# Gate slots of six output tiles: one 512-column matmul for the high weights times [high | low] operand

## The chip, the cores and the metric

The kernel runs on one core of a Trainium2 chip. The metric is device time in microseconds (us) of one execution, median over runs; lower is better. Engines are called by the profile's short names: PE (TensorE, the matmuls), PEld (its weight loads), DVE (VectorE), ACT (ScalarE), POOL (GpSimd) and SP (SyncE, which issues the weight DMAs here). They run side by side and meet at semaphores. TensorE reads SBUF and writes PSUM; DVE and ACT read and write both; POOL works in SBUF.

## The reference, cut to what matters

Two small transformer blocks on 256 tokens of width 1024. The part that the change touches closes the first block's state-space mixer:

```python
    g = jax.nn.gelu(y).astype(h.dtype)
    val, gate = jnp.split(g @ w_glu, 2, axis=-1)
    return val * jax.nn.sigmoid(gate)
...
            x = x + s5_mixer(h, ssm_w_in[i], ...)
        h = rms_norm(x, ffn_norm[i])
        x = x + conv_ffn(h, ffn_w_up[i], ffn_conv_w[i], ffn_conv_b[i], ffn_w_down[i])
```

All of it is fp32. `w_glu` is 1024 x 2048.

## The kernel before

Activations lie transposed: 128 features on the partitions, 256 tokens along the row, eight such tiles (`m` or `k` from 0 to 7) for the 1024 features. All weights come as one stream of 197 slots of 128 x 2048 floats, through a ring of six buffers that SP fills well ahead. A slot holds 16 blocks of 128 x 128 (8 `k` times 2 output halves).

A product in full precision is made of three products of reduced precision (fp32r). ACT rounds the slot into `w_hi` (`high_part`, line 503, one 128x2048 Copy). POOL subtracts that from the slot to get `w_lo` (`low_part`, line 413, four pieces of 128x512), and then tells `w_ready`. The operand is split in the same way into `hi` and `lo`. For each block PE runs `three` (lines 1568 to 1570): `w_hi`*hi, `w_lo`*hi and `w_hi`*lo, 256 columns each, all added into one PSUM bank; that is 48 matmuls a slot. `w_hi` and `w_lo` have three buffers each (`SPLIT`).

The gate stage has slots 4 to 11, one for each output tile: slot 4+m holds the value columns of tile m as half 0 and its gate columns as half 1. Slot 4 is handled whole, slots 5 to 11 with `three`. Slot 5's low part is made by DVE; POOL's first one is slot 6. Slot 12 is the first of the feed-forward stage (ffn0). The order on each engine is written out by hand. In the gate loop, for tile m:

- ACT runs the Copy for `w_hi` of slot 4+m+2 (`high_parts_to(s + 2)`), waits until PE is done with slot 4+m, takes the sigmoid of the gate half (line 650), and waits for `x_ready`. Then `operand_tile` makes the next stage's `hi` tile (line 641) and the square (line 642), and the loop goes on to the next tile's Copy.
- DVE waits for `gated`, multiplies value by sigmoid (line 1158: one input in PSUM, one in SBUF), adds the product to `x` (line 1160: both inputs in SBUF, tells `x_ready`), and makes the `lo` tile (line 972, all in SBUF).
- POOL makes the low part of a slot when ACT's Copy of it has ended; PE starts a slot when its low part is done (`w_ready`) and the slot before it has ended.

In tile 1, ACT also issues a small DMA (`bias_oh`) ahead of the sigmoid; behind slot 8, PE has a small product for the bias table. In tile 7, ACT loads another function table and makes `w_hi` of slot 14 between the sigmoid and the operand tile. Behind the loop it issues the load of `p0` and splits it (`pe_operand`) before it comes to ffn0's norm.

Of the kernel before, what the change touches and what calls it, by code (L numbers as in the profile page):

```python
# [9 lines left out]
P = 128  # L10
D = 1024
T = 256
KT = D // P
# [24 lines left out]
for _name, _n in STAGES:  # L38
# [8 lines left out]
SET = dict(s5=1, ffn0=0, ple0=0, q=1, kv=0, diff=1, ffn1=0, ple1=0, even=1, mixed=1,  # L47
           ffn2=0, odd=0, stick=1, ffn3=0)
# [31 lines left out]
def stick_pair(t):  # L80

    return STICK_AT.index(t) if t in STICK_AT else None
# [97 lines left out]
def program(nc, a, out):  # L180
    f32, f32r = mybir.dt.float32, mybir.dt.float32r
    ALU, ACT, AX = mybir.AluOpType, mybir.ActivationFunctionType, mybir.AxisListType
    ctx = ExitStack()
    with ctx:
        def sb(name, shape, dt=f32):
            return ctx.enter_context(nc.sbuf_tensor(name, shape, dt))
# [16 lines left out]

        with nc.sbuf_tensor("s5_cm", [P, 2, 2, PAIRS, 32], f32) as s5_cm:
            pass
        opnd = [sb("opnd0", [P, 2, KT, T], f32r)]
        opnd.append(sb("opnd1", [P, 2, KT, T], f32r))
        acc = ctx.enter_context(nc.psum_tensor("acc", [P, 4, 512], f32))
        up = [ctx.enter_context(nc.psum_tensor(f"up{i}", [P, 2, T], f32)) for i in range(2)]
        side = ctx.enter_context(nc.psum_tensor("side", [P, 2, 512], f32))  # L210
# [15 lines left out]
        def sem(name):  # L226
            if name not in sems:
                sems[name] = ctx.enter_context(nc.semaphore(name))
            return sems[name]
# [89 lines left out]
        def weights_hi(s):  # L319

            return last_hi[s] if s in last_hi else w_hi[:, s % SPLIT]

        def weights_lo(s):

            return last_lo[s] if s in last_lo else w_lo[:, s % SPLIT]
# [18 lines left out]
        def hi(name):  # L344
            return opnd[SET[name]][:, 0]

        def lo(name):
            return opnd[SET[name]][:, 1]

        block = ctx.enter_context(nc.Block())  # L350

# [125 lines left out]
        def _(act):  # L477
            c = Counts(act, sem)
            A = nc.scalar.activation
# [25 lines left out]
            def high_parts_to(s):  # L505
                while ahead[0] <= min(s, N_SLOTS - 1):
                    high_part(ahead[0])
                    ahead[0] += 1
# [8 lines left out]
            def root_tables():  # L517

                nc.scalar.preload_act_table_set("natural_log_exp_and_others")
# [18 lines left out]
            w = s_small  # L538
# [100 lines left out]
            def operand_tile(name, m):  # L639
                c.wait("x_ready")  # L640
                c.up(A(hi(name)[:, m], x[:, m], ACT.Copy, scale=gain(name, m)), "hi_ready")  # L641
                c.up(A(sq[:, m], x[:, m], ACT.Square), "sq_ready")

            for m in range(KT):
                s = START["glu"] + m
                high_parts_to(s + 2)
                act.wait_ge(sem("mm_done"), s + 1)
                if m == 1:
                    act.dma_start(d_oh, a["bias_oh"]).then_inc(dma["bias_oh"], 16)
                c.up(A(f_gg[:, 0], up[m % 2][:, 1], ACT.Sigmoid), "gated")  # L650
                if m == KT - 1:
                    root_tables()
                    high_parts_to(s + 3)
                operand_tile("ffn0", m)
# [89 lines left out]
            S = START["kvq"]  # L744
# [69 lines left out]
            S = START["evin"]  # L814
# [61 lines left out]
            for n in range(EVEN_STEPS):  # L876
# [16 lines left out]
                if n >= 5 and n % 2:  # L893
                    h = (n - 5) // 2
# [11 lines left out]
            S = START["qkv"]  # L906
# [5 lines left out]
            for t in range(STICK_HALVES):  # L912
# [16 lines left out]
                p = stick_pair(t - 1)  # L929
# [7 lines left out]
                p = stick_pair(t - 3)  # L937
# [5 lines left out]
                p = stick_pair(t - 1)  # L943
# [7 lines left out]
                p = stick_pair(t - 4)  # L951
# [10 lines left out]
        def _(dve):  # L962
            c = Counts(dve, sem)
            V = nc.vector

            def step(ins):
                c.up_and_wait(ins, "dve_step")

            def low_tile(name, m):

                c.wait("hi_ready")
                c.up(V.scalar_tensor_tensor(lo(name)[:, m], x[:, m], gain(name, m), hi(name)[:, m].bitcast(f32),  # L972
                                            ALU.mult, ALU.subtract), "lo_ready")
# [9 lines left out]
            w = s_small  # L983
# [170 lines left out]


            for m in range(KT):
                c.wait("gated")
                step(V.tensor_tensor(f_h[:, 0], up[m % 2][:, 0], f_gg[:, 0], ALU.mult))
                c.tell("up_free")
                c.up_and_wait(V.tensor_tensor(x[:, m], x[:, m], f_h[:, 0], ALU.add), "x_ready")  # L1160
                low_tile("ffn0", m)
                if m == 5:
                    c.wait("bias_ps")
                    c.up_and_wait(V.tensor_copy(d_row, aux[0][0:HEADS, 0:384]), "bias_sb")
# [132 lines left out]
            S, u0 = START["kvq"], BANK["kvq"]  # L1297
# [81 lines left out]
            S, u0 = START["evin"], BANK["evin"]  # L1379
# [88 lines left out]
            for n in range(EVEN_STEPS):  # L1468
# [12 lines left out]
                if n >= 6 and n % 2 == 0:  # L1481
                    h = (n - 6) // 2
# [9 lines left out]
            S, u0 = START["qkv"], BANK["qkv"]  # L1492
# [19 lines left out]
            for t in range(STICK_HALVES):  # L1512
# [4 lines left out]
                p = stick_pair(t - 1)  # L1517
# [6 lines left out]
                p = stick_pair(t - 3)  # L1524
# [7 lines left out]
                p = stick_pair(t - 2)  # L1532
# [7 lines left out]
                p = stick_pair(t - 4)  # L1540
# [9 lines left out]
        def _(pe):  # L1550
            c = Counts(pe, sem)
            MM = nc.tensor.matmul
            used = [0]

            def slot_ready(s, i=None):
                pe.wait_ge(sem("w_ready"), s + 1 if i is None else i * 6 + (s + 1))

            def bank(i=None, loop_uses=0):

                u = used[0]  # L1560
                used[0] += 1
                if u >= 2:
                    pe.wait_ge(sem("up_free"), u - 1 if i is None else i * 4 + (u - 1))
                return up[u % 2]

            def three(o, l_hi, l_lo, r_hi, r_lo, start, stop):

                MM(o, l_hi, r_hi, start=start, stop=False, skip_group_check=True)  # L1568
                MM(o, l_lo, r_hi, start=False, stop=False, skip_group_check=True)  # L1569
                return MM(o, l_hi, r_lo, start=False, stop=stop, skip_group_check=True)  # L1570

            def square_sums(h):

                c.wait("sq_ready", KT // 2)
                for q in range(4):
                    ins = MM(aux[1][QUAD * q:QUAD * q + QUAD, 0:T], ones[:, 0:QUAD], sq[:, 4 * h + q],  # L1576
                             start=(h == 0), stop=(h == 1), tile_position=(0, QUAD * q), skip_group_check=True)
                if h:
                    c.up(ins, "ssq")
# [21 lines left out]
            def up_slot(name, s, i=None, fresh=False, sums=False, fold=False, tokens=0, order=range(KT)):  # L1601

                slot_ready(s, i)
                o = bank(i)
                w_h, w_l = weights_hi(s), weights_lo(s)
                for j, k in enumerate(order):
                    if fresh:
                        c.wait("hi_ready")
                        c.wait("lo_ready")
                    for m in range(2):  # L1610
                        w = slice((2 * k + m) * P, (2 * k + m + 1) * P)
                        ins = three(o[:, m], w_h[:, w], w_l[:, w], hi(name)[:, k], lo(name)[:, k],
                                    k == order[0] and m == 0, k == order[-1])
                    if sums and j == KT // 2 - 1:
                        square_sums(0)
                    between(k, fold, tokens)
                c.up(ins, "mm_done")
                if sums:
                    square_sums(1)

            def begin_slot(s):
                slot_ready(s)
                return bank()
# [71 lines left out]
            S = START["w_in"]  # L1695
# [30 lines left out]
            o = whole_bank(S)  # L1726
# [4 lines left out]
            for m in range(KT):  # L1731
                c.wait("sq_ready")
                ins = MM(aux[1][:, 0:T], ones, sq[:, m], start=(m == 0), stop=(m == KT - 1), skip_group_check=True)
# [65 lines left out]
            o = whole_bank(S + 1)  # L1799
# [6 lines left out]
            o = whole_bank(S + 2)  # L1806
# [9 lines left out]
            o = whole_bank(S + 3)  # L1816
# [10 lines left out]
            S = START["glu"]  # L1827
# [11 lines left out]
            o = whole_bank(S)  # L1839
# [1 line left out]
            s5_out(7)  # L1841
            gelu_part(o, range(4, KT))
            for m in range(1, KT):
                up_slot("s5", S + m, fresh=(m == 1))
                if m == 4:
                    pe.wait_ge(dma["bias_oh"], 16)
                    c.up(MM(aux[0][0:HEADS, 0:384], d_oh[:, 384:384 + HEADS], d_oh[:, 0:384], start=True, stop=True),
                         "bias_ps")
# [50 lines left out]
            S = START["kvq"]  # L1899
# [86 lines left out]
            for t in range(DIFF_HALVES):  # L1986
                i, half = t // 2, t % 2
                if i < 12:
                    if half == 0:
                        o = begin_slot(S + i)  # L1990
# [20 lines left out]
            S = START["evin"]  # L2011
# [125 lines left out]
            S = START["qkv"]  # L2137
# [83 lines left out]
            for t in range(STICK_HALVES):  # L2221
                i, half = t // 2, t % 2
                if i < 12:
                    if half == 0:
                        o = begin_slot(S + i)
# [9 lines left out]
                p = stick_pair(t - 3)  # L2235
                if p is not None:
                    stick_values(p)
                p = stick_pair(t)
# [153 lines left out]
```

## Time and profile before

| | |
|---|---|
| median of 3 runs | 1327.33 us (1327.25 to 1328.0) |
| profiled execution, first to last instruction | 1324.4 us |
| instructions | 27666 |
| PE busy | 1296.3 us, 98% of the span |
| POOL busy | 1006.1 us, 76% |
| ACT busy | 682.9 us, 52% |
| DVE busy | 637.0 us, 48% |
| mean granted TensorE clock | 0.999 of full speed |

The profiled execution is one of its own: its span is 2.9 us shorter than the median run, since a run's time also holds what lies around the instructions. Busy shares are means over stages with different limits. A row of the timeline gives start and length in us from the span's start; a matmul's length is its own latency, and matmuls overlap, so what one costs is read from the distance of starts.

### The profile page before, as it was taken

Reading aid. Unit: us, or ns where it says so; the run is one execution under the profiler, and the core shown is the slowest. Engines: PE = TensorE matmul, PEld = TensorE weight load, DVE = VectorE, ACT = ScalarE, POOL = GpSimd, SP = SyncE. Lnnn points to the kernel's source line nnn. Section 1 sums busy time; section 2 is a strip of 40 time slices with the busy share of each in tenths; the row PEclk is TensorE's granted clock in tenths of the full one; section 3 lists DMA queues with packets and bytes.
Section 4 is the critical chain, followed back from the end, with each engine's and each line's share of the span. In section 5 each row is a group of like instructions: output and inputs, shape, how many; then the busy total and the mean of one; then the engine's idle time right before and its main releaser. Section 6 shows DMA issues by size and latency. Waiting matters only on the chain.

```text
span 1324.4 us, 27666 instructions
## 1 busy us (share of the span) xinstructions
PE 1296.3 (98%) x10976; PEld 1247.4 (94%) x10976; DVE 637.0 (48%) x1163; ACT 682.9 (52%) x944; POOL 1006.1 (76%) x793
## 2 busy tenths in 40 slices
PE   6999999999999999999999999999999999999999
PEld 6889999999988889999999978999999999999998
DVE  8994465555555748455565574211113455311112
ACT  7725643444666756443457565434446566543342
POOL 1327888888777659888887794988887766988885
PEclk9999999999999999999999999999999999999999
DMA  6305675545535235555454532555554433555530
GB/s 269 129 33 181 169 250 191 185 172 181 191 134 185 101 126 183 178 188 188 172 178 160 193 128 96 192 192 179 174 185 167 160 126 120 187 178 187 190 127 32
DMA packets 33879, 217.07 MB, mean 164 GB/s; under 512 B 3683, under 2 KB 7428, under 8 KB 8196
## 3 DMA queue, kind: packets, MB, share of 16 engines
q1 hardware_dynamic: 30096, 211.14, 45.1%
q10 hardware_dynamic: 3700, 4.75, 1.4%
q8 instruction: 60, 0.98, 0.3%
q14 instruction: 23, 0.19, 0.0%
HBM read 213.26 MB, written 2.62 MB: 163 GB/s over the span
## 4 chain that ended last, share of the span: by engine, by line
PE 85%; DVE 6%; ACT 6%; issue 2%; POOL 1%; DMA 0%; DVEq 0%; SPq 0%; ACTq 0%; POOLq 0%
PE up L1568 19%; PE up L1569 18%; PE up L1570 18%; PE acc L1568 7%; PE acc L1570 6%; PE acc L1569 6%; DVE opnd L972 2%; PE side L1795 2%; PE up L1703 1%; PE acc L1761 1%; ACT w_hi L503 1%; ACT opnd L641 1%; PE side L1576 1%; PE up L1834 1%; PE acc L1933 0%
## 5 line engine op out<-in xcount | busy, mean ns | idle before, releaser
L413 POOL TENSOR_TENSOR w_lo<-ring,w_hi 128x512 fp32r<-128x512 f32 x748 | 955.4, 1311 | 235.7 <-ACT w_hi L503 231.8
L1568 PE MATMUL up<-opnd,w_hi 128*128 128x256 f32 x2064 | 592.3, 287 | 3.7 <-DVE opnd L972 1.5
L1569 PE MATMUL up<-opnd,w_lo 128*128 128x256 f32 x2064 | 583.9, 283 | 0.0
L1570 PE MATMUL up<-opnd,w_hi 128*128 128x256 f32 x2064 | 583.8, 283 | 0.0
L503 ACT ACTIVATE w_hi<-ring 128x2048 fp32r<-128x2048 f32 x188 | 358.9, 1910 | 264.4 <-PE up L1570 202.7
L1568 PEld LDWEIGHTS up<-opnd,w_hi 128*128 128x128 f32 x2064 | 395.6, 192 | 16.1 <-issue 13.1
L1569 PEld LDWEIGHTS up<-opnd,w_lo 128*128 128x128 f32 x2064 | 395.8, 192 | 1.3 <-issue 1.0
L1570 PEld LDWEIGHTS up<-opnd,w_hi 128*128 128x128 f32 x2064 | 395.7, 192 | 0.0
L1568 PE MATMUL acc<-opnd,w_hi 128*128 128x256 f32 x784 | 223.0, 284 | 1.2 <-DVE x L1218 1.2
L1569 PE MATMUL acc<-opnd,w_lo 128*128 128x256 f32 x784 | 221.8, 283 | 0.0
L1570 PE MATMUL acc<-opnd,w_hi 128*128 128x256 f32 x784 | 221.8, 283 | 0.0
L1568 PEld LDWEIGHTS acc<-opnd,w_hi 128*128 128x128 f32 x784 | 150.4, 192 | 2.8 <-DVE x L1218 2.1
L1569 PEld LDWEIGHTS acc<-opnd,w_lo 128*128 128x128 f32 x784 | 150.4, 192 | 0.0
L1570 PEld LDWEIGHTS acc<-opnd,w_hi 128*128 128x128 f32 x784 | 150.4, 192 | 0.0
L977 DVE TENSOR_TENSOR side<-up,rstd 128x512 f32<-128x512 f32 x44 | 30.8, 699 | 198.9 <-PE up L1570 189.9
L977 DVE TENSOR_TENSOR mix<-up,rstd 128x512 f32<-128x512 f32 x72 | 49.7, 691 | 144.3 <-PE up L1570 116.0
L664 ACT ACTIVATE opnd<-side 128x256 fp32r<-128x256 f32 x88 | 33.8, 384 | 110.6 <-DVE side L1198 110.6
L972 DVE SCALAR_TENSOR_TENSOR opnd<-x,par,opnd 128x256 fp32r<-128x256 f32 x80 | 66.9, 855 | 24.3 <-ACT opnd L641 19.5
L1198 DVE TENSOR_TENSOR side<-mix,side 128x256 f32<-128x256 f32 x88 | 37.7, 429 | 71.3 <-ACT mix L662 67.0
L1201 DVE TENSOR_TENSOR opnd<-side,opnd 128x256 fp32r<-128x256 f32 x88 | 37.4, 425 | 46.0 <-ACT opnd L664 46.0
L662 ACT ACTIVATE mix<-side 128x256 f32<-128x256 f32 x88 | 33.0, 375 | 51.2 <-DVE side L1189 47.7
L427 POOL TENSOR_TENSOR s_work<-s_work 128x512 f32<-128x512 f32 x7 | 8.9, 1277 | 66.0 <-DVE s_work L1119 35.4
(296 smaller groups left out, 1421.3 us busy)
## 6 DMA issues: line engine op xcount, KB each, us to landing
ring<-in_stream SPq DMA_DIRECT2D x197, 1024.0 KB, 4.9
bias_rows<-mix ACTq DMA_DIRECT2D x1, 1536.0 KB
mix<-in_s_b SPq DMA_DIRECT2D x1, 1024.0 KB, 5.6
x<-in_x SPq DMA_DIRECT2D x1, 1024.0 KB, 7.7
mix<-in_s_c SPq DMA_DIRECT2D x1, 1024.0 KB, 11.7
mix<-bias_rows ACTq DMA_DIRECT2D x1, 1024.0 KB, 5.4
out_x<-x SPq DMA_DIRECT2D x8, 128.0 KB, 1.7
mix<-in_p ACTq DMA_DIRECT2D x2, 256.0 KB, 3.4
```

Source lines behind the costliest of these rows:

```text
L413: ins = nc.gpsimd.tensor_tensor(w_l[:, cols], ring[:, r, cols], w_h[:, cols].bitcast(f32), ALU.subtract)
L503: c.up(A(weights_hi(s), ring[:, s % RING], ACT.Copy), "w_hi_ready")
L662: c.up(A(f_gg[:, 0], gate_ps, ACT.Gelu_apprx_tanh if l < 2 else ACT.Silu), "gated")
L664: c.up(A(opnd[1][:, 0, 2 * parity + part], h_ps, ACT.Copy), "h_hi")
L972: c.up(V.scalar_tensor_tensor(lo(name)[:, m], x[:, m], gain(name, m), hi(name)[:, m].bitcast(f32), ALU.mult, ALU.subtract), "lo_ready")
L977: c.up_and_wait(V.tensor_tensor(dst, up[u][:], rstd[:].unsqueeze(1).broadcast_to([P, 2, T]), ALU.mult), "up_free")
L1198: c.up_and_wait(V.tensor_tensor(h_ps, f_gg[:, 0], val_ps, ALU.mult), "h_raw")
L1201: c.up_and_wait(V.tensor_tensor(hl, h_ps, hh.bitcast(f32), ALU.subtract), "h_ready")
L1568: MM(o, l_hi, r_hi, start=start, stop=False, skip_group_check=True)
L1569: MM(o, l_lo, r_hi, start=False, stop=False, skip_group_check=True)
L1570: return MM(o, l_hi, r_lo, start=False, stop=stop, skip_group_check=True)
L1795: ins = MM(o, s5_cm[:, r, 1 - odd, pair], rhs, start=False, stop=(k == 3), tile_position=(0, 32 * q), skip_group_check=True)
```

## The change

For tiles 1 to 6 (slots 5 to 10), the two products with `w_hi` become one: hi and lo of an operand tile now lie side by side (`both`, 512 columns), and one matmul multiplies `w_hi` with the pair. Its left 256 columns hold `w_hi`*hi, to which `w_lo`*hi is added as before; the right 256 columns hold `w_hi`*lo by itself. So each half of a slot takes a whole PSUM bank (of `acc`, in place of a half of `up`), and the two halves of a result still have to be added. ACT copies the right halves of both banks to SBUF (128x512, `f_c[:, 0:2]`), DVE adds the left halves to them (128x512, to `f_c[:, 2:4]`), and ACT's sigmoid and DVE's multiply then read that sum. Tiles 0 and 7 stay as they were.

```diff
-        opnd = [sb("opnd0", [P, 2, KT, T], f32r)]
-        opnd.append(sb("opnd1", [P, 2, KT, T], f32r))
+        both = [sb("opnd0", [P, KT, 2, T], f32r)]
+        both.append(sb("opnd1", [P, KT, 2, T], f32r))
+        opnd = [v.rearrange("p k h t -> p h k t") for v in both]
...
+        def hi_lo(name):
+            return both[SET[name]]
+
+        def glu_banks(m):
+
+            return acc[:, 2 * (m % 2):2 * (m % 2) + 2]
...
-                c.up(A(f_gg[:, 0], up[m % 2][:, 1], ACT.Sigmoid), "gated")
+                if 0 < m < KT - 1:
+                    c.up(A(f_c[:, 0:2], glu_banks(m)[:, :, T:2 * T], ACT.Copy), "cross_sb")
+                    c.wait("glu_sum")
+                    c.up(A(f_gg[:, 0], f_c[:, 3], ACT.Sigmoid), "gated")
+                else:
+                    c.up(A(f_gg[:, 0], up[m % 2][:, 1], ACT.Sigmoid), "gated")
...
-                c.wait("gated")
-                step(V.tensor_tensor(f_h[:, 0], up[m % 2][:, 0], f_gg[:, 0], ALU.mult))
-                c.tell("up_free")
+                if 0 < m < KT - 1:
+                    c.wait("cross_sb")
+                    c.up_and_wait(V.tensor_tensor(f_c[:, 2:4], glu_banks(m)[:, :, 0:T], f_c[:, 0:2], ALU.add), "glu_sum")
+                    c.tell("up_free")
+                    c.wait("gated")
+                    step(V.tensor_tensor(f_h[:, 0], f_c[:, 2], f_gg[:, 0], ALU.mult))
+                else:
+                    c.wait("gated")
+                    step(V.tensor_tensor(f_h[:, 0], up[m % 2][:, 0], f_gg[:, 0], ALU.mult))
+                    c.tell("up_free")
...
+            def wide_slot(s, o, fresh=False):
+
+                slot_ready(s)
+                bank()
+                w_h, w_l = weights_hi(s), weights_lo(s)
+                for k in range(KT):
+                    if fresh:
+                        c.wait("hi_ready")
+                        c.wait("lo_ready")
+                    for m in range(2):
+                        w = slice((2 * k + m) * P, (2 * k + m + 1) * P)
+                        MM(o[:, m, 0:T], w_l[:, w], hi("s5")[:, k], start=(k == 0), stop=False, skip_group_check=True)
+                        ins = MM(o[:, m], w_h[:, w], hi_lo("s5")[:, k], start=False, stop=(k == KT - 1),
+                                 skip_group_check=True)
+                c.up(ins, "mm_done")
...
-                up_slot("s5", S + m, fresh=(m == 1))
+                if m < KT - 1:
+                    wide_slot(S + m, glu_banks(m), fresh=(m == 1))
+                else:
+                    up_slot("s5", S + m)
```

On ACT, one turn of the gate loop was, from the Copy of a slot's weights to the next one (slots 8 and 9; `mix` is the memory in which `f_gg` and `f_c` lie):

```order
79 L503 ACTIVATE w_hi<-ring 128x2048
80 L650 ACTIVATE mix<-up 128x256
81 L641 ACTIVATE opnd<-x,par 128x256
82 L642 ACTIVATE sq<-x 128x256
83 L503 ACTIVATE w_hi<-ring 128x2048
```

and is now this (line numbers of the changed kernel are 8 to 20 higher on ACT and DVE):

```order
85 L511 ACTIVATE w_hi<-ring 128x2048 [waits mm_done,ring_full2]
86 L659 ACTIVATE mix<-acc 128x512 [waits mm_done]
87 L661 ACTIVATE mix<-mix 128x256 [waits glu_sum]
88 L649 ACTIVATE opnd<-x,par 128x256 [waits x_ready]
89 L650 ACTIVATE sq<-x 128x256
90 L511 ACTIVATE w_hi<-ring 128x2048 [waits mm_done,ring_full3]
```

One instruction of 512 columns and a wait for DVE (`glu_sum`) have come in ahead of the sigmoid; the next slot's Copy (line 511, before 503) still stands behind all of it.

On DVE a tile was:

```order
135 L1158 TENSOR_TENSOR mix<-up,mix 128x256 [waits gated]
136 L1160 TENSOR_TENSOR x<-x,mix 128x256 [waits dve_step]
137 L972 SCALAR_TENSOR_TENSOR opnd<-x,par,opnd 128x256 [waits hi_ready,x_ready]
```

and is now:

```order
135 L1172 TENSOR_TENSOR mix<-acc,mix 128x512 [waits cross_sb]
136 L1175 TENSOR_TENSOR mix<-mix 128x256 [waits glu_sum,gated]
137 L1180 TENSOR_TENSOR x<-x,mix 128x256 [waits dve_step]
138 L985 SCALAR_TENSOR_TENSOR opnd<-x,par,opnd 128x256 [waits hi_ready,x_ready]
```

There is an addition more, and the multiply (line 1175) now reads only `mix`, which is SBUF, where it read `up`, which is PSUM.

## Rows read from the trace of the kernel before

**Rows 1.** Page, the chain that ended last: shares of the span by engine

```profile
PE 85%; DVE 6%; ACT 6%; issue 2%; POOL 1%; DMA 0%; DVEq 0%; SPq 0%; ACTq 0%; POOLq 0%
```

**Rows 2.** Busy time in a stretch: length, then PE, PEld, DVE, ACT, POOL, clock, DMA

```profile
106.00:130.00 24.00, 24.00 (x197) 23.77 (x196) 8.93 (x12) 14.18 (x18) 22.41 (x17) 1.00 0.61 222
```

**Rows 3.** Timeline of PE, starts of gate slots: start, length, line, operation

```profile
107.03 0.28 PE L1569 MATMUL up<-opnd,w_lo 128*128 128x256 f32 x1
107.15 0.28 PE L1570 MATMUL up<-opnd,w_hi 128*128 128x256 f32 x1
...
124.18 0.28 PE L1568 MATMUL up<-opnd,w_hi 128*128 128x256 f32 x1
...
148.15 0.28 PE L1568 MATMUL up<-opnd,w_hi 128*128 128x256 f32 x1
```

**Rows 4.** Timeline of ACT in the gate stage; in brackets the idle time before

```profile
110.62 1.90 ACT L503 ACTIVATE w_hi<-ring 128x2048 fp32r<-128x2048 f32 x1
...
113.47 0.38 ACT L650 ACTIVATE mix<-up 128x256 f32<-128x256 f32 x1 [0.95 <-PE up L1570]
115.46 0.51 ACT L641 ACTIVATE opnd<-x,par 128x256 fp32r<-128x256 f32 x1 [1.60 <-DVE x L1160]
...
116.18 1.90 ACT L503 ACTIVATE w_hi<-ring 128x2048 fp32r<-128x2048 f32 x1
118.62 0.38 ACT L650 ACTIVATE mix<-up 128x256 f32<-128x256 f32 x1 [0.54 <-PE up L1570]
```

**Rows 5.** Timeline of DVE in the gate stage

```profile
113.89 0.42 DVE L1158 TENSOR_TENSOR mix<-up,mix 128x256 f32<-128x256 f32 x1 [2.59 <-ACT mix L650]
114.47 0.95 DVE L1160 TENSOR_TENSOR x<-x,mix 128x256 f32<-128x256 f32 x1 [0.15 <-DVE mix L1158]
...
119.62 1.38 DVE L1160 TENSOR_TENSOR x<-x,mix 128x256 f32<-128x256 f32 x1 [0.15 <-DVE mix L1158]
```

**Rows 6.** Timeline of POOL, single pieces of the low parts

```profile
112.60 1.29 POOL L413 TENSOR_TENSOR w_lo<-ring,w_hi 128x512 fp32r<-128x512 f32 x1
113.84 1.30 POOL L413 TENSOR_TENSOR w_lo<-ring,w_hi 128x512 fp32r<-128x512 f32 x1
115.09 1.48 POOL L413 TENSOR_TENSOR w_lo<-ring,w_hi 128x512 fp32r<-128x512 f32 x1
...
120.67 1.48 POOL L413 TENSOR_TENSOR w_lo<-ring,w_hi 128x512 fp32r<-128x512 f32 x1
```

**Rows 7.** Timeline of PE, two fp32r matmuls of 512 columns and what follows

```profile
1066.56 0.63 PE L2187 MATMUL acc<-mix_r 128*128 128x512 f32 x2
1067.03 0.39 PE L2189 MATMUL acc<-mix_r 128*128 128x256 f32 x2
```

**Rows 8.** Groups by line and shape, DVE: count, busy us, mean ns, idle before

```profile
L1160 DVE TENSOR_TENSOR x<-x,mix 128x256 f32<-128x256 f32 x8 | 7.6, 947 | 1.2 <-DVE mix L1158 1.2
...
L1530 DVE TENSOR_TENSOR mix<-mix,acc 128x512 f32<-128x512 f32 x8 | 5.5, 688 | 4.7 <-PE acc L2191 4.7
...
L1346 DVE SCALAR_TENSOR_TENSOR mix<-mix 128x256 f32<-128x256 f32 x8 | 3.9, 484 | 0.3
...
L1158 DVE TENSOR_TENSOR mix<-up,mix 128x256 f32<-128x256 f32 x8 | 3.4, 424 | 21.5 <-ACT mix L650 21.5
```

**Rows 9.** Groups by line and shape, ACT: a 512-column Copy out of PSUM

```profile
L575 ACT ACTIVATE s_work<-acc 64x512 f32<-64x512 f32 x4 | 2.4, 592 | 3.5 <-PE acc L1719 3.4
```

**Rows 10.** Timeline of ACT at the end of the gate stage

```profile
148.35 0.38 ACT L650 ACTIVATE mix<-up 128x256 f32<-128x256 f32 x1 [1.25 <-PE up L1570]
...
150.04 0.36 ACTq L734 DMA_DIRECT2D mix<-in_p  x1
150.04 1.91 ACT L503 ACTIVATE w_hi<-ring 128x2048 fp32r<-128x2048 f32 x1
...
151.86 0.49 ACT L641 ACTIVATE opnd<-x,par 128x256 fp32r<-128x256 f32 x1
...
154.26 0.72 ACT L698 ACTIVATE opnd<-mix 128x256 fp32r<-128x256 f32 x2 [1.60 <-DMA mix<-in_p]
```

## The prediction

> **What bounds the kernel now.** I read the chain that ended last first: 85% of the span is PE [rows 1], so the kernel ends when PE's matmuls do. The stretch of the gate slots comes next, because a mean says nothing of a stage: from 106 to 130 us PE is busy all the time at the full clock, but POOL is busy 22.41 us of 24.00 too [rows 2]. PE is ahead of the others by a little only, and the question is by how much.
>
> PE's pace: matmuls of 256 columns start 0.12 us apart (107.03, 107.15), so a slot of 48 lasts 5.76 us. Slot 8 starts at 124.18 and slot 12 at 148.15 [rows 3], and nothing but a small product for the bias table stands between.
>
> How weights come to PE: ACT's Copy of slot 7 ends at 110.62 + 1.90 = 112.52 [rows 4], POOL's first piece of it starts at 112.60 [rows 6], 0.08 us later. So POOL waits for ACT, slot by slot. ACT's Copy of slot 8 ends at 116.18 + 1.90 = 118.08 [rows 4]; four pieces, two at 1.25 us from start to start (112.60 to 113.84) and two at 1.44, make 5.4, so slot 8's low part is ready near 123.55, only 0.6 us before PE starts on it at 124.18. I call T(s) the end of ACT's Copy of slot s; w_ready(s) is T(s) + 5.5. That 0.6 us is all that the gate loop of ACT can lose before PE waits.
>
> What ACT's loop consists of: for tile 1, sigmoid at 113.47, operand tile at 115.46, Copy of slot 8 at 116.18 [rows 4]. In the 1.6 us between the first two it waits for DVE: multiply 0.42 (113.89), 0.15 for its own semaphore, addition to `x` 0.95 (114.47) [rows 5].
>
> Why that addition takes 0.95 or 1.38 us: POOL's pieces. It ends at 115.42, which is 0.33 behind the start of a POOL piece at 115.09; the one that starts at 119.62 ends at 121.00, again 0.33 behind a piece, at 120.67 [rows 5, 6]. And these pieces take 1.48 us, not 1.29. So a DVE instruction with both inputs in SBUF waits for the end of the POOL piece that runs, goes between two pieces, and lengthens the next by 0.19. The groups say the same: mean 947 ns for the addition (line 1160), 424 for the multiply that has one input in PSUM (line 1158), 484 for a two-SBUF-input instruction in a stage where POOL rests (line 1346) [rows 8]. The Trainium skill, "SBUF — State Buffer", section "SBUF: two separate sides", has this rule: GpSimd and a VectorE instruction with two SBUF inputs take one port pair as an exclusive lock for a whole instruction. By that rule, the trace agrees.
>
> **The change, part by part.** *PE.* Two matmuls of 256 columns go, one of 512 comes. Two fp32r matmuls of 512 columns occupy 1066.56 to 1067.03, 0.235 us each [rows 7], against 2 x 0.12 = 0.24 [rows 3]. A slot of 16 blocks falls from 5.76 to 16 x (0.12 + 0.235) = 5.68 us, at most 0.5 us over six slots. PE pays by column, so one weight load fewer is worth almost nothing.
>
> *ACT and DVE, per tile of 1 to 6.* New, ahead of the sigmoid: a Copy of 512 columns out of PSUM, 0.59 us (line 575, half the partitions [rows 9]; not under the 0.38 that 256 columns take [rows 4]), and DVE's addition of 512 columns with one input in PSUM, 0.69 (line 1530 [rows 8]), with about 0.04 us at each hand-over (sigmoid's end 113.85 to multiply at 113.89 [rows 4, 5]). That is 1.36 us on the chain. The multiply stays 256 wide, but now reads `f_c` and `f_gg`, both in SBUF, so it falls under the wait for POOL's piece, as line 1160 does. Then the addition to `x` comes 0.15 us after it, inside the next piece, and waits for that one's end as well.
>
> *One turn of ACT's loop, from T on.* An ACT instruction behind another starts 0.09 before that one's listed end (151.86 against 150.04 + 1.91 [rows 10]). Copy -0.09 to 0.50; addition 0.54 to 1.23; sigmoid 1.27 to 1.67 (0.38 from PSUM; I take 0.40 from SBUF); multiply ready at 1.71. POOL's pieces start at 0.08, 1.33 and 2.58, so the multiply waits until 2.58 and ends 2.90. Addition to `x` ready at 3.05; the third piece, lengthened, ends the wait at 4.02, and it is done at 4.34. Operand tile 4.38; the next Copy starts 0.72 later (115.46 to 116.18 [rows 4]), at 5.10, and ends at 7.00. **The loop takes 7.0 us a tile, and PE needs 5.68.** ACT, not PE, sets the pace, and POOL follows it (5.5 of 7.0). What is queued behind the wait on ACT is the Copy of the next slot's weights, and POOL and then PE wait for that.
>
> *Tile 1.* T(7) = 112.52 stays. Copy at 113.47 to 114.06, addition to 114.79, sigmoid to 115.23, multiply ready at 115.27: just behind the piece that starts at 115.09 [rows 6], so it waits for 116.34 and ends 116.66. Addition to `x` from 116.81: that piece ends 117.78, done 118.10; operand tile 118.14, Copy 118.86, T(8) = 120.76 instead of 118.08. PE's slot 6 is done by then (sigmoid at 118.62 before [rows 4]), so ACT goes on without a pause: T(9) = 127.76, T(10) = 134.76, T(11) = 141.76, T(12) = 148.76, T(13) = 155.76.
>
> *PE.* Slot 8 starts at T(8) + 5.6 = 126.4 (was 124.18), slot 12 at 154.4 (was 148.15): **6.2 us late**. In between PE idles 1.3 us a slot, and the shorter slots only lengthen that; the 0.5 us buys nothing. Slot 5's own start, and ACT's, are as before.
>
> *Behind it.* Tile 7's sigmoid comes at 155.7 instead of 148.35, 7.3 late, so the DMA of `p0`, issued 1.7 us behind it, lands, and its split (154.26 [rows 10]) runs, 7.3 late where PE is 6.2 late. ACT's norm stands behind that split, so between 0 and 1.1 us come on top; I take 0.4, because before the change the norm could wait some tenths without PE noticing. From there PE bounds as before (98% busy over the span), and nothing gives time back.
>
> *Sum.* 6.2 + 0.4 = 6.6 us. The profiled span would go from 1324.4 to 1331.0; the median of runs is 2.9 above the span, so 1327.3 + 6.6 = **1333.9 us**.
>
> *Bounds.* The Copy may cost 0.38 to 0.68; in the steady turn the multiply is then ready between 1.50 and 1.80, still between the pieces at 1.33 and 2.58, so the period doesn't move: waits come in steps of a piece. In tile 1 it decides: 0.18 us quicker and the multiply catches 115.09, T(8) is 1.25 earlier, and the sum 5.0 to 5.4. Above: with the whole 1.1 from `p0`, 7.3. Case by case 1332.3 to 1334.6.
>
> **The rivals.** *A: the multiply isn't held by POOL* (its place is line 1175 of the changed kernel, its price 0.42). Then the addition to `x` is ready at 2.28 and catches 2.58; the period is 5.56, under PE's 5.68. In tile 1, T(8) is 119.3, slot 8's low part is ready at 124.85, 0.7 late; later slots don't wait, and six shorter slots take back up to 0.4: +0.3 to +0.5, **1327.7**, no slowdown that shows. It decides at the second piece that is waited for. Against it: line 1160 at 947 ns against 424 with PSUM. For it: its two inputs and its output lie close together in one tile, which I have no row for. 10%.
>
> *B: in part.* The multiply finds POOL idle or catches the first piece in some of the tiles, as hand-overs are shorter than 0.04 us or pieces lie otherwise: some tiles at 5.75, others at 7.0; three of six gives about +3, **1330.3**. 9%.
>
> *C: faster.* The 512-column matmul costs no more than one of 256 and the new steps are hidden. Then a slot takes 16 x 0.24 = 3.84 us, but PE can't have slot 11 ahead of its low part, which before came 2.1 us ahead of PE: **1325.2**. That is hardly 0.2% and needs rival A too. The Trainium skill, "TensorE: Matmul & The Clock Gate", section "Back-to-back issue gap", speaks for such a price, with about 131 ns for 512 columns in a stream against 81 for 128. The fp32r matmuls here take 235 [rows 7], and the measurement decides. 2%.
>
> *D: more.* One more piece waited for in each turn, or a slow clock in PE's new pauses: 6 x 1.25 = 7.5 on top, **1341**. 4%.
>
> **How the numbers follow.** The forecast, ACT's loop as the bound in all six tiles, has 75%. The range 1330.0 to 1336.5 holds it, most of B, and up to 2.6 us of further pauses above; it leaves out A, C, D and a little of B, some 18%. About 0.2% (2.65 us) is what a measurement of this kernel can tell from no change. Faster by more than that: 1%. Within: A, nearly all of C, a third of B, 14%. Slower: the rest, 85%.
>
> **What would show it.** In the profile after: the wide matmul and the next start 0.235 us apart; PE's idle time in the gate stage is ended by POOL's low part, about 1.3 us a slot from slot 8 on; ACT's Copies of slots 8 to 13 end 7.0 us apart; line 1175 takes 0.9 to 1.2 us and ends 0.33 behind the start of a POOL piece, and so does line 1180; slot 12 starts 6.2 us later. I am wrong if line 1175 takes 0.42, or if ACT's Copies follow PE's pace, or if the time lost at slot 12 comes back in ffn0.

## The result and the profile after

| | median | runs |
|---|---|---|
| before, same chip | 1327.29 us | 4 (1326.36 to 1328.0) |
| changed kernel | 1333.31 us | 4 (1332.82 to 1334.16) |

The ratio is 1.0047 (95% interval 1.0033 to 1.0061): the change costs 6.0 us. The forecast was 1333.9. The profiled execution has a span of 1332.4 us and is the longest of the four (1334.16 us); 8.0 us lie between the two spans, 6.0 between the medians. A run's time is 1.8 us above its own span here, so of the 2.9 us between span and median before the change only 1.8 lies around the instructions: the execution profiled before was a short one, and it stands against a long one.

The page first. The chain of work that ended last, and the group of POOL's low parts (count, busy us, mean ns; then the idle time before them and what ended it):

```profile
PE 83%; DVE 8%; ACT 6%; issue 2%; POOL 1%; DMA 0%; DVEq 0%; ACTq 0%; SPq 0%; POOLq 0%
...
L421 POOL TENSOR_TENSOR w_lo<-ring,w_hi 128x512 fp32r<-128x512 f32 x748 | 954.9, 1310 | 243.8 <-ACT w_hi L511 240.8
```

PE gives two hundredths of the chain to DVE [rows 1]. POOL's idle time ahead of the low parts is 243.8 us where it was 235.7, and what ACT's Copy ended of it 240.8 where it was 231.8. Over the whole kernel PE is busy about as long as before (1298.9 us against 1296.3), so shares can't say where 6 us went. The waits of PE from 107 to 165 us can (total, times, longest):

```profile
PE acc L1652 <- POOL w_lo L421: 2.2, 1, 2.2
PE up L1588 <- POOL w_lo L421: 2.0, 2, 1.1
PE up L1588 <- DVE opnd L985: 1.1, 1, 1.1
```

In the kernel before this list is empty for the stage. Three of the four waits are for a slot's low part, which is what the prediction said; the fourth, for tile 7's operand, it did not see. The places in the timeline of PE (start, length of one):

```profile
124.20 0.40 PE L1653 MATMUL acc<-opnd,w_hi 128*128 128x512 f32 x1
126.76 0.52 PE L1652 MATMUL acc<-opnd,w_lo 128*128 128x256 f32 x1 [2.16 <-POOL w_lo L421]
...
147.72 0.39 PE L1588 MATMUL up<-opnd,w_hi 128*128 128x256 f32 x1 [1.05 <-POOL w_lo L421]
...
154.71 0.39 PE L1588 MATMUL up<-opnd,w_hi 128*128 128x256 f32 x1 [0.98 <-POOL w_lo L421]
...
160.48 0.28 PE L1590 MATMUL up<-opnd,w_hi 128*128 128x256 f32 x1
161.88 0.36 PE L1588 MATMUL up<-opnd,w_hi 128*128 128x256 f32 x1 [1.12 <-DVE opnd L985]
```

Slot 8 starts at 126.76, slot 11 at 147.72, slot 12 at 154.71, where the kernel before had 124.18 and 148.15 for slots 8 and 12 [rows 3]. Gate slot 5 began at 106.72 before and at 107.21 here (0.49 later, ahead of all that the change touches), so slot 12 is (154.71 - 107.21) - (148.15 - 106.72) = 6.07 us late. Behind it one pause more: 161.88 - 160.48 = 1.40 us between two starts that otherwise lie 0.12 apart, 1.28 lost. 0.49 + 6.07 + 1.28 = 7.84 of the 8.0 us between the spans.

Why the low parts are late is one turn of ACT's loop. The chain of work in order of time, from 119 to 128 us (start, us on the chain):

```profile
119.05 0.40 ACT sq L650
119.45 1.81 ACT w_hi L511
121.26 0.48 ACT mix L659
121.75 0.02 issue
121.77 0.70 DVE mix L1172
122.47 0.02 issue
122.50 0.43 ACT mix L661
122.92 0.02 issue
122.95 1.23 DVE mix L1175
124.18 0.02 issue
124.20 1.39 DVE x L1180
125.59 0.02 issue
125.61 0.03 ACT opnd L649
125.64 0.39 issue
126.03 0.40 ACT sq L650
126.43 1.80 ACT w_hi L511
```

No PE and no POOL stand in it: weights for slot 8 (L511), the new Copy (L659), the new addition (L1172), sigmoid, multiply (L1175), addition to `x` (L1180), squares of the operand tile, and then L511 again at 126.43, 6.98 us after the last. The chain of this stretch used to be PE matmul behind PE matmul. Now look at POOL in the same stretch, single pieces:

```profile
122.59 1.29 POOL L421 TENSOR_TENSOR w_lo<-ring,w_hi 128x512 fp32r<-128x512 f32 x1
123.84 1.46 POOL L421 TENSOR_TENSOR w_lo<-ring,w_hi 128x512 fp32r<-128x512 f32 x1
```

The multiply could begin at 122.95 and ends at 122.95 + 1.22 = 124.17, 0.33 behind the start of the piece at 123.84; that piece is long (1.46) as the lengthened ones of before were [rows 6]. Before, the multiply had one input in PSUM and took 0.42 [rows 5].

### The profile page after: what moved, and what is told of

Read it like the earlier page. It is cut to its first block, busy times and chain, and to the rows that moved or that the text cites. A ratio compares the mean times of both kernels' runs of the same rounds, so it can differ in the third digit from the quotient of the medians.

```text
span 1332.4 us, 27486 instructions
## 1 busy us (share of the span) xinstructions
PE 1298.9 (97%) x10880; PEld 1244.0 (93%) x10880; DVE 647.8 (49%) x1169; ACT 685.9 (51%) x950; POOL 1005.7 (75%) x793
## 4 chain that ended last, share of the span: by engine, by line
PE 83%; DVE 8%; ACT 6%; issue 2%; POOL 1%; DMA 0%; DVEq 0%; ACTq 0%; SPq 0%; POOLq 0%
PE up L1588 18%; PE up L1589 17%; PE up L1590 17%; PE acc L1588 7%; PE acc L1590 6%; PE acc L1589 6%; PE up L1739 2%; DVE opnd L985 2%; ACT w_hi L511 2%; PE side L1831 2%; PE acc L1797 1%; ACT opnd L649 1%; PE side L1596 1%; PE up L1870 1%; PE acc L1972 0%
## 5 line engine op out<-in xcount | busy, mean ns | idle before, releaser
L421 POOL TENSOR_TENSOR w_lo<-ring,w_hi 128x512 fp32r<-128x512 f32 x748 | 954.9, 1310 | 243.8 <-ACT w_hi L511 240.8
L1588 PE MATMUL up<-opnd,w_hi 128*128 128x256 f32 x1968 | 565.1, 287 | 6.8 <-DVE opnd L985 2.6
L1589 PE MATMUL up<-opnd,w_lo 128*128 128x256 f32 x1968 | 556.7, 283 | 0.0
L1590 PE MATMUL up<-opnd,w_hi 128*128 128x256 f32 x1968 | 556.6, 283 | 0.0
L511 ACT ACTIVATE w_hi<-ring 128x2048 fp32r<-128x2048 f32 x188 | 358.9, 1910 | 264.5 <-PE up L1590 202.9
L1588 PEld LDWEIGHTS up<-opnd,w_hi 128*128 128x128 f32 x1968 | 377.2, 192 | 19.3 <-issue 13.7
L1589 PEld LDWEIGHTS up<-opnd,w_lo 128*128 128x128 f32 x1968 | 377.4, 192 | 1.2 <-issue 1.0
L1590 PEld LDWEIGHTS up<-opnd,w_hi 128*128 128x128 f32 x1968 | 377.3, 192 | 0.0
L985 DVE SCALAR_TENSOR_TENSOR opnd<-x,par,opnd 128x256 fp32r<-128x256 f32 x80 | 67.3, 860 | 24.5 <-ACT opnd L649 19.4
```

The costliest lines, as they stand in the source:

```text
L421: ins = nc.gpsimd.tensor_tensor(w_l[:, cols], ring[:, r, cols], w_h[:, cols].bitcast(f32), ALU.subtract)
L511: c.up(A(weights_hi(s), ring[:, s % RING], ACT.Copy), "w_hi_ready")
```

## The experiments

Two batches; in the first the kernel before took 1326.66 us (27 runs, 1326.01 to 1327.85), in the second 1326.88 (21 runs, 1326.05 to 1327.62). "Late" below is read at one row that all kernels have, the norm's first sums over `sq` in slot 12, counted from slot 5's start; before, that distance is 151.12 - 106.72 = 44.40 us.

| kernel | median us (runs) | ratio, 95% interval | norm's sums less slot 5 | late |
|---|---|---|---|---|
| new layout alone | 1326.59 (10) | 1.0000 (0.9991 to 1.0009) | 152.16 - 107.78 | 0.0 |
| wide matmul split | 1334.48 (4) | 1.0058 (1.0042 to 1.0073) | 158.70 - 108.14 | 6.2 |
| sum in PSUM | 1328.55 (11) | 1.0013 (1.0004 to 1.0022) | 153.35 - 107.41 | 1.5 |
| sum in PSUM, weights first | 1326.58 (11) | 0.9999 (0.9990 to 1.0008) | 151.50 - 107.89 | -0.8 |
| changed kernel again | 1333.38 (4) | 1.0054 (1.0039 to 1.0070) | 156.30 - 106.86 | 5.0 |
| weights first | 1326.43 (10) | 0.9999 (0.9990 to 1.0008) | 151.63 - 108.03 | -0.8 |
| half pieces | 1330.08 (10) | 1.0025 (1.0015 to 1.0034) | 154.39 - 107.03 | 3.0 |
| tile 7's operand first | 1333.12 (5) | 1.0049 (1.0035 to 1.0062) | 156.35 - 106.86 | 5.1 |

**The new layout alone**, in the kernel before: hi and lo side by side, three matmuls as ever.

```diff
-        opnd = [sb("opnd0", [P, 2, KT, T], f32r)]
-        opnd.append(sb("opnd1", [P, 2, KT, T], f32r))
+        both = [sb("opnd0", [P, KT, 2, T], f32r)]
+        both.append(sb("opnd1", [P, KT, 2, T], f32r))
+        opnd = [v.rearrange("p k h t -> p h k t") for v in both]
```

> The kernel before with the operands' new layout alone (hi and lo of a tile side by side); no instruction more or less. My theory (the changed kernel loses its 6 us because ACT's gate loop takes 7.0 us a tile, as DVE's multiply and addition each wait for a POOL piece) expects no change: 1327.3 us, within 2 us, PE's slots 5.76 us. A rival, that the new layout costs PE or DVE something at every use of the operands, expects a good part of the 6 us here: 1330 us or more.

1326.59 against 1326.66 us: the layout costs nothing.

**The wide matmul split** in the changed kernel: the same sums in the same banks and the same work on ACT and DVE, but two matmuls of 256 columns.

```diff
-                        ins = MM(o[:, m], w_h[:, w], hi_lo("s5")[:, k], start=False, stop=(k == KT - 1),
+                        MM(o[:, m, 0:T], w_h[:, w], hi("s5")[:, k], start=False, stop=(k == KT - 1), skip_group_check=True)
+                        ins = MM(o[:, m, T:2 * T], w_h[:, w], lo("s5")[:, k], start=False, stop=(k == KT - 1),
                                  skip_group_check=True)
```

> The changed kernel with its 512-column matmul split again into two of 256 columns with the same weights; banks, Copy, additions and order stay. My theory says that PE isn't what is waited for in these slots, so the time stays that of the changed kernel, 1333.3 us, within 1.5 us, with ACT's Copies still 7.0 us apart and less idle time on PE. A rival, that the wide matmul is what slows PE (pauses, or a slow clock), expects a return towards 1327; one that it saves PE time that counts expects 1334 or more.

1334.48 us, no faster than the change, and as late in slot 12: ACT's Copies are 6.96 to 7.00 us apart from tile 2 on, and PE waits for low parts at the same three places (1.9 us in one, 1.9 in two, where it was 2.2 and 2.0). So the form of PE's work isn't what makes slot 12 late; what is left for that is on ACT and DVE. By the time alone the rival that put 1334 or more on a saving of PE isn't excluded: the median is 1.1 to 1.2 us above those of the changed kernel, and the intervals overlap. In the profile it isn't seen: the spans lie 0.9 us apart (1333.3 and 1332.4), and slot 5 already starts 0.93 later (108.14 and 107.21), ahead of everything in which the two kernels differ.

**The sum in PSUM**: DVE's addition writes over the left halves of the banks, and sigmoid and multiply read them there. As many instructions of the same sizes, but the multiply has one input in PSUM again.

```diff
-                    c.up(A(f_gg[:, 0], f_c[:, 3], ACT.Sigmoid), "gated")
+                    c.up(A(f_gg[:, 0], glu_banks(m)[:, 1, 0:T], ACT.Sigmoid), "gated")
...
-                    c.up_and_wait(V.tensor_tensor(f_c[:, 2:4], glu_banks(m)[:, :, 0:T], f_c[:, 0:2], ALU.add), "glu_sum")
-                    c.tell("up_free")
+                    sums = glu_banks(m)[:, :, 0:T]
+                    c.up_and_wait(V.tensor_tensor(sums, sums, f_c[:, 0:2], ALU.add), "glu_sum")
                     c.wait("gated")
-                    step(V.tensor_tensor(f_h[:, 0], f_c[:, 2], f_gg[:, 0], ALU.mult))
+                    step(V.tensor_tensor(f_h[:, 0], glu_banks(m)[:, 0, 0:T], f_gg[:, 0], ALU.mult))
+                    c.tell("up_free")
```

> The changed kernel, but DVE's 512-column addition leaves its sum in PSUM, so that the sigmoid and the multiply read PSUM, and the multiply again has one input there; Copy, addition and their hand-overs all stay. My theory: the multiply takes 0.42 us and waits for no piece of POOL; the loop falls from 7.0 to 5.56 us, a little under PE's slot of 5.6; tile 1 still costs some 1 us, and the shorter slots give some tenths back: 1327.3 to 1328.2 us, and a multiply of 0.42 us in the profile. The rival, that the Copy and the addition on the chain (1.4 us a tile) are what costs and not the multiply's wait, expects 1331 to 1333.

1328.55 us, 1.9 above the kernel before: most of the cost is gone, and this is what separates the theory from a cost of the added instructions as such. The timeline of its DVE in the turn of tile 2:

```profile
120.54 0.70 DVE L1173 TENSOR_TENSOR acc<-acc,mix 128x512 f32<-128x512 f32 x1 [1.74 <-ACT mix L659]
121.77 0.42 DVE L1175 TENSOR_TENSOR mix<-acc,mix 128x256 f32<-128x256 f32 x1 [0.52 <-ACT mix L661]
122.35 0.58 DVE L1181 TENSOR_TENSOR x<-x,mix 128x256 f32<-128x256 f32 x1 [0.16 <-DVE mix L1175]
```

The multiply takes 0.42 where the change took 1.22, and the addition to `x` is in time for the end of the piece in which the multiply ran (0.58 where it was 1.38). ACT's Copies of weights start at 111.31, 118.13, 123.69, 129.25, 136.03, 142.84 and 148.41, which is 5.56 apart or 6.8: a turn catches a piece or waits for one more. PE waits twice for low parts, 0.8 us each; I put the 0.35 us above the expected range down to the turns of 6.8, on the profile's word alone.

The Trainium skill, "SBUF — State Buffer", section "SBUF: two separate sides", words it as an exclusive lock on the port pair that GpSimd and a VectorE instruction with two SBUF inputs share, held for a whole instruction. The two kernels bear it out from both sides: 1.22 us with two inputs in SBUF, 0.42 with one in PSUM, same shape, same place.

**The sum in PSUM, weights first**: besides, ACT makes the next slot's weights between its Copy and its wait for DVE's sum.

```diff
                     c.up(A(f_c[:, 0:2], glu_banks(m)[:, :, T:2 * T], ACT.Copy), "cross_sb")
+                    high_parts_to(s + 3)
                     c.wait("glu_sum")
```

> As the kernel that leaves the sum in PSUM, and ACT makes the high part of the next slot between its 512-column Copy and the sigmoid, not behind the operand tile. My theory: the Copy for the next weights no longer waits for DVE, POOL runs ahead of PE, ACT's turn is 4.9 us, and PE's slots of some 5.6 us set the pace: six slots shorter by 0.1 to 0.2 us, 1326.2 to 1327.0 us, and no idle time of PE ended by POOL's low part in slots 7 to 11. A rival, that PE itself is slower in wide slots, expects 1328 or more.

1326.58 us, no difference from before, with all of the new work still there. PE waits nowhere in the stage, and POOL has one row for 32 pieces:

```profile
108.21 43.09 POOL L421 TENSOR_TENSOR w_lo<-ring,w_hi 128x512 fp32r<-128x512 f32 x32 [18.23 <-ACT w_hi L511]
```

Slot 12's row comes 0.8 us earlier than before. Slots 7, 9 and 10 take 5.64 to 5.66 us from one to the next where three matmuls of 256 columns took 5.76, so I read this as PE's own saving; no run takes it apart from the rest. A median with an interval of 0.2% can't show it.

**The changed kernel again**, in the second batch, unedited.

> The changed kernel once more, as the measure for the three beside it. Expected 5.5 to 7.5 us over the kernel before, as measured already (6.0 by the medians).

1333.38 us, the same. Its profile differs in tile 1 from the first one, and this was one of the bounds of the prediction. DVE's multiply and POOL's piece behind it here:

```profile
115.24 0.42 DVE L1175 TENSOR_TENSOR mix<-mix 128x256 f32<-128x256 f32 x1 [0.48 <-ACT mix L661]
```
```profile
115.26 1.56 POOL L421 TENSOR_TENSOR w_lo<-ring,w_hi 128x512 fp32r<-128x512 f32 x1
```

and in the first profile of the same kernel:

```profile
115.59 1.59 DVE L1175 TENSOR_TENSOR mix<-mix 128x256 f32<-128x256 f32 x1 [0.48 <-ACT mix L661]
```
```profile
115.61 1.29 POOL L421 TENSOR_TENSOR w_lo<-ring,w_hi 128x512 fp32r<-128x512 f32 x1
```

In both the multiply came 0.02 us ahead of the piece's listed start; once it went first, once it waited out the piece, at 1.17 us. What decides between the two, the listed times don't show. From there on both run at 7.0 us a turn (ACT's Copies at 117.86, 124.85, 131.86, 138.84, 145.82, 152.81 here), one 1.1 us behind the other at slot 12.

**Weights first**, with the sum in SBUF as in the change.

```diff
                     c.up(A(f_c[:, 0:2], glu_banks(m)[:, :, T:2 * T], ACT.Copy), "cross_sb")
+                    high_parts_to(s + 3)
                     c.wait("glu_sum")
```

> The changed kernel, with ACT's high part of the next slot moved between the 512-column Copy and the sigmoid; the sum stays in SBUF and the multiply still waits for a POOL piece. My theory: that wait then delays x, hi and lo, but not the weights; POOL runs ahead of PE, ACT's turn is about 6.3 us against PE's 5.6, so tile 7's operand comes some 3 us late and PE waits for it once, at the end of ffn0's first slot: 1.2 to 2.5 us over the kernel before. The rival, that the multiply's wait costs PE directly by its length wherever it stands, expects 4 us or more over it.

Missed: 1326.43 us, as before the change, where I expected a cost. I had taken the multiply's wait to stay as it was and to lengthen the turn. The rows of ACT and DVE:

```profile
120.66 1.91 ACT L511 ACTIVATE w_hi<-ring 128x2048 fp32r<-128x2048 f32 x1
...
126.24 1.91 ACT L511 ACTIVATE w_hi<-ring 128x2048 fp32r<-128x2048 f32 x1
```
```profile
122.90 0.67 DVE L1176 TENSOR_TENSOR mix<-mix 128x256 f32<-128x256 f32 x1 [1.42 <-ACT mix L662]
123.61 1.40 DVE L1181 TENSOR_TENSOR x<-x,mix 128x256 f32<-128x256 f32 x1
```
```profile
123.25 1.48 POOL L421 TENSOR_TENSOR w_lo<-ring,w_hi 128x512 fp32r<-128x512 f32 x1
...
124.68 1.48 POOL L421 TENSOR_TENSOR w_lo<-ring,w_hi 128x512 fp32r<-128x512 f32 x1
...
126.12 1.48 POOL L421 TENSOR_TENSOR w_lo<-ring,w_hi 128x512 fp32r<-128x512 f32 x1
```

Both DVE instructions are still held: they end at 123.57 and 125.01, 0.32 and 0.33 behind the pieces at 123.25 and 124.68. But no weights stand behind them, POOL never pauses (one row of 32 pieces, 44.19 us), and a turn is 5.58 us, which is four pieces of POOL, three of them lengthened (1.25 from start to start, and 1.43 or 1.44 three times: the operand tile's low part is held too). Two later turns take 6.1 and 6.3 us, and PE still waits nowhere. Since POOL no longer starts afresh at T(s), the multiply doesn't meet its pieces where it did; here it falls near the end of one. So a held DVE instruction costs here only what is queued behind it.

**Half pieces**: POOL makes the low parts of slots 6 to 13 in eight pieces of 256 columns, nothing else in the change is touched. If the wait is for a piece, it must shrink with the piece.

```diff
-                for q in range(QUARTERS):
-                    cols = slice(q * 2048 // QUARTERS, (q + 1) * 2048 // QUARTERS)
+                n = 2 * QUARTERS if START["glu"] <= s < START["ffn0"] + 2 else QUARTERS
+                for q in range(n):
+                    cols = slice(q * 2048 // n, (q + 1) * 2048 // n)
```

> The changed kernel, with POOL's low parts of slots 6 to 13 in eight pieces of 256 columns, not four of 512. My theory: each of DVE's two waits ends at the next piece, so they shrink by about 0.6 us each at most; ACT's Copies come about 5.9 us apart, not 7.0, if POOL's pieces take about 0.7 us: 1 to 3 us over the kernel before. If a piece of 256 columns takes 0.75 us or more, POOL itself needs 6 us a slot and it is 3 us or more. The rival, that DVE's multiply and addition are slow for another reason than the piece that runs (two SBUF inputs as such), expects no gain: 5.5 us or more over it, and line 1175 as long as before.

1330.08 us, 3.2 over the kernel before: half of the cost. In the turn of tile 2 the multiply takes 0.80 where it took 1.22, and still ends 0.33 behind the start of a piece (121.63 + 0.80 = 122.43 against 122.10):

```profile
121.63 0.80 DVE L1176 TENSOR_TENSOR mix<-mix 128x256 f32<-128x256 f32 x1 [0.48 <-ACT mix L662]
122.46 0.85 DVE L1181 TENSOR_TENSOR x<-x,mix 128x256 f32<-128x256 f32 x1
```
```profile
121.41 0.74 POOL L422 TENSOR_TENSOR w_lo<-ring,w_hi 128x256 fp32r<-128x256 f32 x1
122.10 0.93 POOL L422 TENSOR_TENSOR w_lo<-ring,w_hi 128x256 fp32r<-128x256 f32 x1
```

A turn is 6.0 to 6.1 us, twice 6.8 (ACT's Copies at 111.23, 118.05, 124.07, 130.19, 136.31, 143.13, 149.15). The time is just above the 1 to 3 us that I expected: half pieces start 0.69 us apart, so two of them take 1.38 where a whole one takes 1.25, and POOL itself is slower.

**Tile 7's operand first**: to test the fourth wait, tile 7's operand tile goes ahead of the table load and of the weights of slot 14.

```diff
+                operand_tile("ffn0", m)
                 if m == KT - 1:
                     root_tables()
                     high_parts_to(s + 3)
-                operand_tile("ffn0", m)
```

> The changed kernel, with ACT's operand tile of tile 7 ahead of the table load and of the high part of slot 14. In the changed kernel's profile PE waits 1.4 us at the end of ffn0's first slot, for tile 7's lo part, which DVE made in 1.56 us behind a POOL piece. My theory: that wait goes, 1.0 to 1.4 us under the changed kernel, and slot 14's weights, 1 us later, still come in time. The rival, that the late load of p0 and ACT's norm behind it set this stretch (as I forecast, with 0.4 us), expects no gain over 0.5 us.

Here L985 runs at 157.06 in 0.77 us, PE has no such wait, and slot 13's first row is at 160.55 where the changed kernel of the same batch had 161.87. Nearly all of this 1.3 us is still there at the end of the profile: both start slot 5 at 106.86, and the spans are 1329.8 and 1331.0 us. The medians don't show it: 1333.12 against 1333.38, a gain of 0.3 where I expected 1.0 to 1.4 and the rival no more than 0.5. Each profile is of the shortest run of its kernel (1331.57 and 1332.75), and both multiplies caught their piece in tile 1; how the other runs went there isn't known. So the profile shows what the fourth wait was for, and by the time it stays open whether 1.2 us or 0.3 is gained.

## Why the prediction was right, and where it was off

*PE.* Right: after the wide matmul the next start is 0.23 us away (123.50 to 123.73, 123.85 to 124.08), so a block is 0.35 us against 0.36, and slot 12 comes 0.8 us earlier where nothing else sets the pace (the two kernels with the weights first); the prediction had at most 0.5. It bought nothing in the change. Rival C's price, a wide matmul at the 0.12 us of one of 256, is wrong: it takes 0.23. The Trainium skill, "TensorE: Matmul & The Clock Gate", section "Back-to-back issue gap", gives about 131 ns for 512 columns in a stream; these fp32r ones take 230, and the measurement decides.

*ACT's loop.* Right: 7.0 us predicted, 6.96 to 7.01 measured between L511's starts (119.36, 126.33, 133.29, 140.30, 147.29, 154.28). Copy 0.57 (predicted 0.59), addition 0.69 (0.69), sigmoid from SBUF 0.42 (0.40), multiply 1.14 to 1.22 behind tile 1 (1.19: held to 2.58, then 0.32), addition to `x` 1.38 to 1.40. That the multiply is held is what rival A denied; the sum in PSUM and the half pieces show it by taking the cause away in two ways.

*Slots 8 and 12.* T(8) was put at 120.76 and is 121.26, which the later start (0.49) makes up; in the second profile it is 119.76, where the lower bound was 120.76 - 1.25 = 119.51. Slot 12 was put 6.2 late and is 6.07, in the second profile 4.95 by the same reckoning (153.24 - 106.86 less 41.43). The prediction had 6.2 for a multiply that misses its piece in tile 1, and 5.0 as the bound for one that catches it; both came.

*The tail.* Mis-sized, and its cause was wrong. I put 0.4 us on the split of `p0` and the norm behind it. The `p0` load landed in time (its split, L711, ran at 160.48 without a wait). ACT's lag from which I worked is there: tile 7's sigmoid starts at 156.08, 7.73 us later than before, where slot 12 is 6.56 later. But it reaches PE by tile 7's operand tile, which stands behind the table load and the weights of slot 14. What PE waited for, 1.28 us, was the low part of that tile, held by POOL's piece:

```profile
160.17 1.56 DVE L985 SCALAR_TENSOR_TENSOR opnd<-x,par,opnd 128x256 fp32r<-128x256 f32 x1 [2.35 <-ACT opnd L649]
```
```profile
160.19 1.26 POOL L421 TENSOR_TENSOR w_lo<-ring,w_hi 128x512 fp32r<-128x512 f32 x1
```

It came 0.02 us before the piece's listed start and waited it out. Before the change it took 0.48 us, as POOL rested just then (from 152.41 to 153.56):

```profile
152.47 0.48 DVE L972 SCALAR_TENSOR_TENSOR opnd<-x,par,opnd 128x256 fp32r<-128x256 f32 x1 [2.47 <-ACT opnd L641]
```

So 1.56 - 0.48, some 1.1 of the 1.28 us, is the hold. The prediction had the rule that holds it and did not apply it to this instruction.

*Rival D's slow clock* did occur in the first profile, and by slot 11 it had cost nothing. PE's row by stretches (length, busy of PE, PEld, DVE, ACT, POOL, granted clock, DMA share, GB/s), changed kernel:

```profile
122.70:126.70 4.00, 1.90 (x11) 1.39 (x9) 3.06 (x3) 1.30 (x4) 4.00 (x3) 1.00 0.01 4
126.70:130.10 3.40, 3.34 (x11) 2.86 (x12) 1.17 (x3) 2.42 (x3) 1.80 (x3) 0.52 0.67 193
130.10:134.00 3.90, 3.90 (x23) 3.31 (x21) 3.19 (x3) 1.43 (x3) 3.59 (x3) 0.98 0.25 105
```

After the pause of 2.56 us (from start to start, 124.20 to 126.76) PE is granted 0.52, close to the lower of its levels (1.2 of 2.4 GHz), for 3.4 us, and its blocks start 0.64 us apart (127.50, 128.14) instead of 0.35. No wait is listed at slot 9, since PE itself was late there; but weights come every 7.0 us and a slot needs 5.7, so by slots 11 and 12 PE was waiting again, and their starts are set by the low parts. In the second profile, at the full clock, each of the slots 8 to 12 begins behind a pause of 1.46 to 1.58 us between starts: that is the 1.3 us of idle time a slot of the prediction, which in the first profile the slow clock took up at slot 9 and for the most part at slot 10.

*The sum.* 6.6 us predicted. The two profiles have 6.07 + 1.28 = 7.35 and 4.95 + 1.3 = 6.25; the medians 6.0 and 6.5. That the forecast lies within 0.6 us of both medians is in part luck: its tail was 0.9 too small, and in the profile that took the predicted way through tile 1 the sum is 0.75 above it.

## What to carry to other kernels

Before an instruction is put between two engines' hand-overs, look at what is queued behind the wait on each of them: here 0.6 us of slack stood against six turns that grew from 5.6 us (one of them 6.8) to 7.0, and moving the weight Copy ahead of the wait made the same work free. On a VectorE instruction beside a busy GpSimd count the inputs in SBUF: the second one made 0.42 us into 1.2, and keeping one in PSUM took most of the cost away. One fp32r matmul of 512 columns costs nearly what two of 256 do (0.23 us against 0.24), so it is not worth a sum afterwards; here even the best arrangement gained 0.8 us in the stage and nothing that the time shows.

## What the runs showed that I had not expected

- A pause of 2.56 us, behind a stage at full clock, was followed by 3.4 us at 0.52. In the split kernel the 3.4 us behind a pause of 2.2 us show 0.69, which is a mean of both levels: 0.95 from 127.6 to 129 us, 0.50 from 129 to 131. A pause of 1.54 us in the second profile of the changed kernel was followed by the full clock. First the split kernel's stretch behind the pause, then that one:

```profile
127.60:131.00 3.40, 3.32 (x20) 3.33 (x21) 1.16 (x3) 2.45 (x3) 1.80 (x3) 0.69 0.63 195
```
```profile
125.20:129.20 4.00, 3.92 (x22) 3.47 (x23) 1.75 (x3) 2.45 (x3) 2.39 (x3) 1.00 0.72 246
```

- Which of DVE and POOL goes first can't be read from the listed times when they lie 0.02 us apart, and it moves DVE by a whole piece: 1.17 us in tile 1, where slot 12 is 6.07 or 4.95 us late by it. At tile 7 DVE waited in both profiles. The times of the changed kernel (1332.82, 1332.85, 1333.77, 1334.16 and, in the second batch, 1332.75, 1332.82, 1333.95, 1335.04) leave room for two such ways; the profiles are of 1334.16 (late in tile 1) and 1332.75 (in time). That the other runs divide so isn't shown.
- Waits that come in steps of a piece can lock one engine's turn to another's: with POOL never pausing, ACT's turn was 5.56 to 5.58 us in three turns of the kernel with the weights first, and POOL's four pieces in one of them took 127.56 - 122.00 = 5.56. It was so before the change too: ACT's Copies of slots 7 to 11 are 5.54 to 5.57 us apart, while POOL's pieces stand in one row of 24 (32.99 us).
